# Loading the expert-output stage's first slots at the end of the stage before, and merging the first two stages of a two-block kernel

## What is computed

```python
def first_block(x, ...):
    cos, sin = _rope_tables(x.shape[1])          # positions x inverse frequencies
    for l in range(DEPTH):                       # 2 layers
        x = _layer(x, cos, sin, norm_g[l], w_in[l], ...)
def _layer(x, cos, sin, norm_g, w_in, ...):
    h = _rms_norm(x, norm_g)
    proj = h @ w_in                              # 1024 x 2592, then three branches
    ...
def second_block(x, ...):
    for i in range(DEPTH):
        ...                                      # a mixer
        h = rms_norm(x, norm_g[i, 1]) * (1.0 + sc2) + sh2
        x = x + g2 * peer_ffn(h, peer_w_q[i], peer_keys[i], peer_u[i], peer_v[i])
def peer_ffn(h, w_q, sub_keys, u_tab, v_tab):    # 16384 experts, 8 heads x 16 chosen
    ...
    act = jax.nn.gelu(jnp.einsum('thkd,td->thk', u, hx))
    return jnp.einsum('thk,thkd->td', g * act, v_tab[idx])
```

## Time and profile before

| what | value |
|---|---|
| median of 3 runs | 2425.04 us |
| the profiled execution's own time | 2436.46 us |
| its span, first to last instruction | 2434.8 us |
| mean granted TensorE clock, share of full | 0.975 |
| busy: PE / PE weight load / DVE / ACT / POOL | 94% / 82% / 73% / 51% / 12% |
| the 1536 matmuls of each layer's expert outputs (L2736), together | 702.3 us |
| idle of PE just before them, both layers | 20.8 us |
| mean DMA rate over the span | 204 GB/s |

### The profile page before, as it was taken

The page is one execution under the profiler, slowest core; times in us unless marked ns, Lnnn a source line. Parts: engine busy times, 40 slices in busy tenths (PEclk is TensorE's granted clock), DMA queues, the critical chain, the costliest instruction groups (busy, mean ns, idle before and its releaser), DMA issues. The chain is left out here.

```text
span 2434.8 us, 46373 instructions
## 1 busy us (share of the span) xinstructions
PE 2296.0 (94%) x15836; PEld 1995.4 (82%) x15836; DVE 1767.4 (73%) x3166; ACT 1235.9 (51%) x1973; POOL 298.0 (12%) x285
## 2 busy tenths in 40 slices
PE   7989989987999999998999998899999999999998
PEld 6657747964799999996888887589999998788886
DVE  5774775776568887886667778567887887677776
ACT  4643543565444455554445444734446555445454
POOL 0000000000000000002334530000000000353442
PEclk9999999998999999998999999999999999999999
DMA  7555464766347766557777875245776664777775
GB/s 203 191 192 161 165 227 140 277 227 258 122 151 227 227 214 207 186 166 213 242 242 239 243 250 199 104 156 155 229 226 211 202 186 150 253 241 240 242 239 177
DMA packets 247735, 497.92 MB, mean 205 GB/s; under 512 B 58041, under 2 KB 134073, under 8 KB 244305
## 3 DMA queue, kind: packets, MB, share of 16 engines
q1 hardware_dynamic: 247632, 496.55, 64.0%
HBM read 461.82 MB, written 34.65 MB: 204 GB/s over the span
## 5 line engine op out<-in xcount | busy, mean ns | idle before, releaser
L2736 PE MATMUL psum<-split_operands 128*128 128x512 f32 x3072 | 702.3, 391 | 20.8 <-ACT split_operands L2715 20.8
L2736 PEld LDWEIGHTS psum<-split_operands 128*128 128x128 f32 x3072 | 580.0, 189 | 142.6 <-ACT split_operands L2715 21.1
L2472 PE MATMUL psum<-split_operands 128*128 128x256 f32 x4096 | 541.4, 285 | 8.9 <-ACT split_operands L2506 8.8
L2472 PEld LDWEIGHTS psum<-split_operands 128*128 128x128 f32 x4096 | 508.5, 191 | 10.4 <-ACT split_operands L2506 10.4
L2700 POOL TENSOR_TENSOR arena<-arena,residual_gates 128x256 f32 (+1 forms) x256 | 284.0, 1109 | 1730.9 <-DMA residual_gates<-expert_activations 1730.9
L2727 DVE TENSOR_TENSOR split_operands<-weights_ring,split_operands 128x1024 fp32r<-128x1024 f32 x256 | 314.2, 1227 | 204.6 <-ACT split_operands L2715 204.6
L2715 ACT CAST split_operands<-weights_ring 128x1024 fp32r<-128x1024 f32 x256 | 269.5, 1053 | 349.6 <-PE psum L2736 347.8
L2549 DVE TENSOR_TENSOR split_operands<-weights_ring,split_operands 128x1024 fp32r<-128x1024 f32 x256 | 313.2, 1224 | 99.7 <-ACT split_operands L2506 98.9
L347 PE MATMUL psum<-split_operands 128*128 128x256 f32 x2496 | 309.6, 286 | 10.2 <-DVE split_operands L363 6.9
L347 PEld LDWEIGHTS psum<-split_operands 128*128 128x128 f32 x2496 | 304.2, 193 | 17.8 <-DVE split_operands L363 8.4
L2476 PE MATMUL psum<-split_operands 128*128 128x256 f32 x2048 | 288.0, 283 | 0.0
(11 more groups left out here) (320 smaller groups left out, 2014.9 us busy)
## 6 DMA issues: line engine op xcount, KB each, us to landing
weights_ring<-in_peer_u_dram SPq DMA_DIRECT2D x256, 512.0 KB, 3.6
weights_ring<-in_peer_v_dram SPq DMA_DIRECT2D x256, 512.0 KB, 4.4
expert_activations<-residual_gates SPq DMA_DIRECT2D x256, 128.0 KB, 1.8
residual_gates<-expert_activations SPq DMA_DIRECT2D x256, 128.0 KB, 4.1
split_words<-in_w_ada_dram SPq DMA_DIRECT2D x20, 768.0 KB, 6.8
weights_ring<-in_w_in_dram SPq DMA_DIRECT2D x6, 2048.0 KB, 8.9
weights_ring<-in_hg_w_in_dram SPq DMA_DIRECT2D x5, 2048.0 KB, 8.4
arena<-in_hg_w_in_dram SPq DMA_DIRECT2D x5, 2048.0 KB, 8.0
```

The lines of the kernel that those rows point to most:

```text
L2472: nc.tensor.matmul(K.ps[:, 4 + b, 0:SEQ], u_t[:, b, 0, k], h[:, wh, k], start=(k == 0 and wh == 0), stop=False)
L2736: return K.nc.tensor.matmul(K.ps[:, 4 + 2 * t + half], g[:, s, w, t * P:(t + 1) * P], vs[:, s % 2, wv, half * 512:(half + 1) * 512], start ...
```

## The change

It has four parts.

1. `stage_rope_tables` is no stage any more. Its DVE and ACT work runs in `stage_setup`, once POOL has made the positions and the frequencies have landed on a semaphore of their own.
2. SP in `stage_setup` issues the frequencies first, then `x`, then block 0 of `w_in`; the stage waits for `x` and not for block 0, whose landing is counted on a semaphore of its own that outlives the stage. In layer 0's projection SP issues only block 1 at that place, waits for block 0 and passes its landing on, and goes on to the parameters.
3. `Handover.act` without a tail takes the square root of the first 128 tokens right after their squares.
4. In `stage_expert_inputs` the last four stores are interleaved with loads for the next stage: as a ring slot's last `peer_u` chunk is split, the `peer_v` chunk of the same slot is loaded; as the store out of an activation slot has landed, activations of chunk 0 to 3 are loaded into it. `ExpertOutputs.sp` begins at chunk 4, and ACT casts the rows of chunk 0 before its gated activations.

```diff
         if self.tail is None:
             for t in range(TT):
                 self.act_squares(act, t)
-            for t in range(TT):
                 self.act_root(act, t)
...
+        rope_tables(K, block, sem, zeroed, invf_loaded)
 
         @block.sync
         def _(sp):
+            sp.dma_start(K.invf[:], K.i["inv_freq"].broadcast_to([P, HALF])).then_inc(invf_loaded, 16)
             sp.dma_start(K.x[:], K.i["x"].rearrange("b (t p) d -> p (b t) d", p=P)).then_inc(loaded, 16)
-            sp.dma_start(K.invf[:], K.i["inv_freq"].broadcast_to([P, HALF])).then_inc(loaded, 16)
-            sp.wait_ge(loaded, 32)
+            _, c0, width = IN_BLOCKS[0]
+            sp.dma_start(K.wslot[0][:, :, 0:width], K.i["w_in"][0, :, c0:c0 + width].rearrange(
+                "(k p) n -> p k n", p=P)).then_inc(K.first_loaded, 16)
+            sp.wait_ge(loaded, 16)
...
+    @block.vector
+    def _(dve):
+        link = Link(dve, chain)
+        dve.wait_ge(pos_made, 1)
+        dve.wait_ge(invf_loaded, 16)
...
-                product.load(sp, n, i["w_in"][bass.ds(l, 1), :, c0:c0 + width].rearrange(
-                    "a (k p) n -> p (a k) n", p=P))
+                if tail is not None or n > 0:
+                    product.load(sp, n, i["w_in"][bass.ds(l, 1), :, c0:c0 + width].rearrange(
+                        "a (k p) n -> p (a k) n", p=P))
+                if tail is None and n == 1:
+                    sp.wait_ge(K.first_loaded, 16)
+                    sp.sem_inc(product.w_loaded[0], 16)
...
+            def reload(s):
+                sp.wait_ge(a_stored[s], NKEYS // SLOTS * 16)
+                sp.dma_start(K.a[:, s], K.act_dram[s:s + 1].rearrange("a p t -> p (a t)")
+                             ).then_inc(K.a_loaded[l][s], 16)
+
             for s in range(SLOTS):
                 sp.sem_inc(u_loaded[s], 16)
             pipeline(sp, SLOTS, NKEYS, SLOTS, load, straight=False)
-            for n in range(NKEYS - SLOTS, NKEYS):
-                store(n, n % SLOTS)
             for s in range(SLOTS):
-                sp.wait_ge(a_stored[s], NKEYS // SLOTS * 16)
+                sp.wait_ge(ut_low, NKEYS - SLOTS + s + 1)
+                sp.dma_start(values[:, s], K.expert_rows(l, s)).then_inc(K.v_loaded[l][s], 16)
+                store(NKEYS - SLOTS + s, s)
+                if s > 0:
+                    reload(s - 1)
+            reload(SLOTS - 1)
...
-        pipeline(sp, 0, NKEYS, SLOTS, load)
+        pipeline(sp, SLOTS, NKEYS, SLOTS, load, straight=False)
...
+        def chunk(n, s, early):
+            if early and n == 0:
+                values(n, s, early)
+                gates(n, s)
+            else:
+                gates(n, s)
+                values(n, s, early)
```

More of the change, by code:

```diff
@@ L435, in _, with rope_tables @@
             pool.wait_ge(made, 2)
-def stage_rope_tables(K, S):
+def rope_tables(K, block, sem, pos_made, invf_loaded):
     nc = K.nc
@@ L445, in stage_rope_tables @@
     low = float(np.float32(two_pi - hi - mid))
[L446 to L475, removed]
@@ new lines, in rope_tables @@
+    chain, angle_ready, sin_done = sem("chain"), sem("angle_ready"), sem("sin_done")
+    area = Area(K.arena)
+    ang, turns, red, whole = (area.take(TT, HALF) for _ in range(4))
+    whole_i = whole.bitcast(I32)
+    @block.vector
[3 more added lines that the diff above has]
+        dve.wait_ge(invf_loaded, 16)
+        for t in range(TT):
+            link(nc.vector.tensor_scalar(ang[:, t], K.invf[:], K.pos[:, t:t + 1], None, ALU.mult))
+        for n, (table, shift) in enumerate(((K.sin, 0.0), (K.cos, 0.25))):
+            link(nc.vector.tensor_scalar(turns, ang, 1.0 / two_pi, shift, ALU.mult, ALU.add))
+            link(nc.vector.tensor_copy(whole_i, turns))
+            link(nc.vector.tensor_copy(turns, whole_i))
+            link(nc.vector.scalar_tensor_tensor(red, turns, -hi, ang, ALU.mult, ALU.add))
+            link(nc.vector.scalar_tensor_tensor(red, turns, -mid, red, ALU.mult, ALU.add))
+            link(nc.vector.scalar_tensor_tensor(red, turns, -low, red, ALU.mult, ALU.add))
+            if shift:
+                link(nc.vector.tensor_scalar(red, red, float(np.pi / 2), None, ALU.add))
+            link(nc.vector.tensor_scalar(table[:], red, float(-np.pi), float(np.pi), ALU.max, ALU.min))
+        dve.sem_inc(angle_ready, 1)
@@ L480, with _ @@
+    @block.scalar
+    def _(act):
+        act.wait_ge(angle_ready, 1)
+        nc.scalar.activation(K.sin[:], K.sin[:], ACT.Sin)
+        nc.scalar.activation(K.cos[:], K.cos[:], ACT.Sin).then_inc(sin_done, 1)
+        act.wait_ge(sin_done, 1)
 IN_BLOCKS = [("cols", 0, 512), ("cols", C_CQ, 512), ("cols", C_CQ + 512, 512),
@@ L2431, in stage_expert_inputs @@
         u = K.ring[:].rearrange("p (s k e) -> p s k e", s=SLOTS, k=KD)
+        values = K.ring[:].rearrange("p (s d) -> p s d", s=SLOTS)
         u_t = K.split[:, 4 * D:].rearrange("p (b w k e) -> p b w k e", b=2, w=2, k=KD)
@@ L2668, in __init__ @@
         self.K = K
-        self.table = K.i["peer_v_2"][l].rearrange("(i j) d -> j i d", j=NKEYS)
-        self.v_loaded = [sem(f"v_loaded{s}") for s in range(SLOTS)]
-        self.a_loaded = [sem(f"a_loaded{s}") for s in range(SLOTS)]
+        self.l, self.v_loaded, self.a_loaded = l, K.v_loaded[l], K.a_loaded[l]
         self.v_high, self.v_low, self.g_high, self.g_low = sem("v_high"), sem("v_low"), sem("g_high"), sem("g_low")
@@ L2706, in act, with gates, values @@
         nc = self.K.nc
-        def chunk(n, s, early):
+        def gates(n, s):
             act.wait_ge(self.weighed, n + 1)
             nc.scalar.copy(self.g[:, s, 0], self.gated(n)).then_inc(self.g_high, 1)
+        def values(n, s, early):
             act.wait_ge(self.v_loaded[s], slot_loads(n, s))
@@ L2893, in memory @@
     K.out_loaded = nc.alloc_semaphore("out_weights_loaded")
+    K.first_loaded = nc.alloc_semaphore("first_weights_loaded")
+    K.v_loaded, K.a_loaded = ([[nc.alloc_semaphore(f"{name}_loaded{l}_{s}") for s in range(SLOTS)]
+                               for l in range(DEPTH)] for name in ("expert_rows", "activations"))
+    K.expert_rows = lambda l, n: K.i["peer_v_2"][l].rearrange("(i j) d -> j i d", j=NKEYS)[bass.ds(n, 1)].rearrange(
+        "a i d -> i (a d)")
     K.hg_out_loaded = [nc.alloc_semaphore(f"hg_out_weights_loaded{m}") for m in range(2)]
@@ L2906, in build @@
         stage_setup(K, S)
-        stage_rope_tables(K, S)
         first_block(K, S)
```

11 lines of the change are left out of this document (4 added, 7 removed).

## The result

The changed kernel took 2404.76 us (median of 6 runs, 2400.82 to 2412.53) against 2427.58 (6 runs, 2424.72 to 2430.12) beside it: ratio 0.9909, 95% interval 0.9896 to 0.9921, so 22.1 us less (19.2 to 25.2). Six more runs in the second group of experiments had a median of 2403.88. The forecast was 2405.0 us and 20.05 us less, counted from 2425.04.

The account below looks back on a forecast made before the run. It took TensorE's expert-output matmuls (702.3 us) to bound the kernel, leaving only idle gaps to win: 3.3 + 1.25 + 2.2 + 1.4 + 6.6 + 5.3 = 20.05 us off 2425.04, giving 2405.0 us; 8-in-10 range 2401 to 2411.5.

Parts of the forecast that it names:

- The start of the stage: First projection: with frequencies issued first and one barrier fewer, its stage starts at 7.85 instead of 11.11, gaining 3.3 us.
- Rival (b): Kernel start: frequencies land no sooner than `x` did, the stage starts 2.5 us later; 2407.5 us, chance 0.08.
- The root: First projection: two squares instead of four before the table load and root, so transposes start earlier, gaining 1.25 us.
- The first weights: First projection: block 0, queued behind `x`, lands about 11.4, so TensorE's gap before the products goes, gaining 2.2 us.
- rival (a): First projection: parameters bind, block 2 reaches TensorE at 44.1, a stall of 3.1 us; 2408.1 us, chance 0.13.
- The clock at the start: First products: without the gap before them TensorE avoids half speed, gaining 1.4 us (0 to 1.4).
- The seams: Ahead of both layers' expert outputs: early loads start TensorE sooner, gaining 6.6 us in the first and 5.3 in the second.
- The clock in the seams: First expert-output matmuls: remaining gaps of 4.6 and 4.2 us won't spare the half clock, so no gain counted.
- Rival (d): Both seams: the clock is spared, half of 4.70 us won in each; 2400.3 us, chance 0.05.
- (c): Both seams: the last store lands behind the rows, costing 2.2 us twice; 2409.4 us, chance 0.09.
- (e): Expert outputs: chunk 4 comes late and the gain is merely put off, 6.6 and 5.3 lost; 2416.9 us, chance 0.02.
- (f): Expert-output loop: landings over 8.3 us make every chunk late, at 9.3 costing 62 us; 2467 us, chance 0.02.

Follow-up runs that it names:

- e12: Changed kernel with `x` issued ahead of the frequencies again, block 0 still behind them; products start at 22.04, 2413.7 us once.
- e7: Changed kernel with the first root back behind all the squares; 2406.73 us.
- e4: Kernel before with only the first root moved right behind the first two squares; 2425.79 us.
- e6: Changed kernel with block 0 of the weights issued at the head of the projection stage again, as before; 2407.4 us.
- e1: Kernel before with only the seam loads changed, the start as before; 2415.80 us, ratio 0.9942 to the kernel before.
- e3: Kernel before, run again without any edit; 2427.48 us in 12 runs, ratio 0.9995.
- e5: Changed kernel with ACT casting the gated activations of chunk 0 before its rows, as before; 2409.75 us once.
- e2: Kernel before with only the changes to the start (tables, early loads, root), seams as before; 2419.46 us, ratio 0.9959.
- e9: Changed kernel, run and profiled again without any edit; 2403.88 us, ratio 0.9907 to the kernel before.
- e10: Changed kernel with each seam's last two activation reloads moved into the next stage, ahead of its small loads; 2403.71 us, ratio 0.9902 to the kernel before.
- e8: Changed kernel with each seam's last two activation reloads moved into the next stage, behind its small loads; 2404.33 us, ratio 0.9897 to the kernel before.

## Why the prediction was right

**The start of the stage: right in kind, 3.3 was 2.7.** The frequencies landed 2.9 us after their issue, not 2.3; the rest of the step held (DVE's chain and two sines, 3.70 to 7.94, are the 4.24 us). The four terms of the stage's start add up to 7.83, not 7.85, which changes nothing. The bounds, 0.8 to 3.9, rested on rows of other loads. Rival (b), frequencies as late as `x`, didn't come, and e12 shows what it would have cost: with the two issues swapped the stage started at 12.33, 3.9 us later, more than the 2.5 that the rival was priced at.

**The root: right, 1.2 for 1.25**, from e7 (19.34 against 18.14), and nothing without the early weights (e4). The trace has the root at 11.09, right behind the 1.28 us of table load from 9.79, and the load right behind the squares. By the Trainium skill, ScalarE: Activation LUTs, section What ACT_TABLE_LOAD costs, a drain of about 1.38 us would have stood there; neither the trace nor e7 shows it. The prediction's 18.8 us was also worked out wrongly: the kernel before and the changed one both have one table load ahead of the first root, so a drain with it would stand in both and leave the gain as it is.

**The first weights: right.** The gap went, and e6 brings it back. The estimate of their landing was early, though: 12.7 (11.0 after 1.74), not 11.4. `x` itself landed 5.4 us after its issue behind the frequencies, at 6.7 instead of 6.1, and block 0 took 6.0 us from there, not 5.3. ACT asked for them at 13.08, so only 0.3 us was left where the text had 1.3. The products started at 18.14, forecast 17.7: 6.3 us gained and not 6.75. Block 2 was issued at 27.44 (28.1) and TensorE ran through (rival (a) fell).

**The clock at the start: 1.4 us, but not in each execution.** Of the five profiles with 2.2 to 3.8 us of idle before the first products four show the fall to 1.2 GHz there (the first of before, e1, e4, e6) and e3 does not; of the nine without that idle none does (e5 and e7 to e12, e2 and the first of the changed kernel). So 1.4 is the price in most runs, some 1.1 in the mean.

**The seams: 6.6 and 5.3 forecast, 6.7 and 4.6 measured in the first pair of profiles.** Over the kernels with and without part 4 the idle is 11.3 and 9.2 on average in one group (before, e2, e3, e4) and 4.4 and 4.5 in the other (changed, e1, e6, e7, e9, e12), so 6.9 and 4.7. Two steps were off by a little each. POOL starts 0.44 us after SP and ACT in the stage, so it and not ACT's cast of rows is what ACT's second cast waits for: 2.27 from the stage's start and not 2.03. And the time from the end of gelu to the next stage was put at 0.43 more for the added reload. In the first seam it was 2.29 to 2.68 (mean 2.58) without part 4 and 2.56 to 2.94 (mean 2.66) with it, in the same kernels; in the second seam 2.29 to 2.30 without and 2.58 to 3.10 (mean 2.73) with it. So the 0.43 is right for the second seam and nearly absent in the first, where the time varied as much before; no run tells why.

**The clock in the seams: as forecast, nearly.** Windows on the first matmuls of the experts, the changed kernel, its second profile (e9), and e10, columns as in the earlier trace rows:

```profile
1090.71:1095.40 4.69, 4.69 (x11) 3.73 (x12) 3.87 (x4) 1.27 (x3) 3.02 (x3) 0.50 0.78 147
```

```profile
1083.70:1088.40 4.70, 4.70 (x14) 3.71 (x15) 4.41 (x4) 1.30 (x4) 2.90 (x3) 0.64 0.78 148
```

```profile
1083.39:1088.09 4.70, 4.70 (x21) 3.88 (x22) 4.41 (x5) 2.73 (x5) 2.62 (x3) 1.00 0.71 58
```

The first is the earlier trace rows again, 11 matmuls at 0.50. In e9 the stretch at half clock was shorter (3.4 us), and in the first seam of e10 it never fell. TensorE was busy at half clock for 5.0 us a seam on average in the kernels without part 4, for some 4 with it: 0.5 us a seam is won. Rival (d), half of 4.70 won in each, did not come: in all 14 seams of the seven profiles with part 4 as in the change, or with only ACT's order undone (e5), the half clock covered 3.4 to 5.1 us of TensorE's work. With e8 and e10 it is 18 seams, and the clock was spared in one of them, e10's first, where the idle was 3.42.

**The sum.** Measured by the traces: 6.3 at the start and 1.1 for its clock, 6.9 + 4.7 in the seams and 1 for theirs, 20.0 us; forecast 20.05. The times say 22.1 (19.2 to 25.2). What lies between, 2 us, no run settles, and the interval nearly reaches down to the sum. It can be chance: the twelve runs of the changed kernel lie over 12.4 us (2400.82 at a mean clock of 0.987, 2413.23 at 0.981), and in its two profiles the falls of the clock that differ stand in stages that the change doesn't touch. That the time itself came within 0.3 us of the forecast is partly luck: the kernel before took 2427.58 in these runs and not 2425.04, and the gain was larger than forecast by nearly as much. Within the sum the errors also cancel, the start and the second seam having won less than forecast and the first seam and the clock in the seams more.

The two first profiles show how single profiles mislead. Their difference is 24.0 us at the end but 14.5 already at 603, where only the start, 6.3 us and its clock, is changed; against e3, the second profile of the kernel before, it is 4.5 at the same instruction.

The other rivals are settled by the trace. The last store did not hold the stage's start by 2.2 us in both seams (c). Chunk 4's activations were 1.44 us late for POOL in the first seam, but TensorE did not wait for them (e). And the loop is no slower (f), the 3072 matmuls taking 701.7 us with 9.4 us of idle. Of the signs that the prediction named, the idle in the second seam, 4.88, lay outside its 4.2 to 4.7, and the first issue (8.43) and the transposes (11.96) came some 0.6 us late.

## What to carry to other kernels

Where a stage's first loads wait for a barrier, move all of those that the first consumer needs: here the rows alone won 2 of 7 us, because the small activations, loaded side by side with them, then ended last. When two loads share a queue and one starts a long chain of small operations, issue that one first; the swap of two lines was worth 3.9 us with a third load queued behind them. And a gain in front of a wait (the root) is only there once the wait is gone, so price edits in the order in which they uncover each other.

## What was unexpected in the hardware

- A load of 64 bytes to each of 128 partitions took 2.8 us ahead of a 1 MB load, 4.5 us behind it, and 6.2 us behind it with a 2 MB load right after.
- DVE's low part of a chunk's rows (128x1024) took 1.75 us while POOL's products ran back to back, and 1.21 in e8 while POOL stood idle. The Trainium skill, SBUF — State Buffer, section SBUF: two separate sides, has a DVE operation with two inputs in SBUF and a GpSimd operation that reads SBUF exclude each other; the two durations agree that they get in each other's way. TensorE shows no idle for it here.
- POOL began 0.44 us after SP and ACT in the stage after the barrier, in the seams in which it had nothing to wait for (1088.88 against 1088.44, 2048.12 against 2047.68).
- After idle times of 2.2 to 3.8 us at the same place the granted clock fell in four of five profiles. The places where it falls largely recur from one execution to the next, but not all of them in each. The run-to-run scatter of 8 to 12 us goes with it: over the 12 executions of the changed kernel the time and the share of clock withheld have a correlation of 0.94, and over the 52 of the kernel before whose clocks were recorded 0.91.
